# V transposed in bulk beside the last two projection tiles, kept by token in DRAM and loaded per chunk of the scan

## What is computed

```python
z = h @ p['w_in']
...
zc = centred_shift(zc, p['mu'])
r, k, v, lw, la = jnp.split(zc, [W_C, 2 * W_C, 3 * W_C, 3 * W_C + N_DIR * LORA_W], -1)
...
def step(s, inp):
    r_t, w_t, k_t, v_t, kk_t, a_t = inp
    sa = jnp.einsum('bhvk,bhk->bhv', s, kk_t)
    s = (s * w_t[:, :, None, :] - sa[..., None] * (kk_t * a_t)[:, :, None, :]
         + v_t[..., None] * k_t[:, :, None, :])
    return s, jnp.einsum('bhvk,bhk->bhv', s, r_t)
...
out = jnp.concatenate([ya, yb, yc], -1) @ p['w_out']
x = x + gate * rms_norm(out, p['g_post'])
```

## Time and profile before

| | us |
|---|---|
| median of 3 runs | 1105.39 |
| lowest, highest | 1103.64, 1105.43 |
| profiled execution | 1102.38 |
| its span | 1100.7 |
| PE busy | 1007.3 (92%) |
| DVE busy | 644.0 (59%) |
| ACT busy | 427.1 (39%) |
| POOL busy | 406.1 (37%) |

### The profile page before, as it was taken

One profiled execution on the slowest core, in us unless ns is written; L12 is line 12 of the kernel. 1 busy time (PEld: TensorE's weight loads), 2 busy tenths in 40 slices (PEclk: granted clock), 3 DMA queues, 4 the chain that ended last, 5 costly groups with the idle time before them and its releaser, 6 DMA issues. The chain is left out here.

```text
span 1100.7 us, 32049 instructions
## 1 busy us (share of the span) xinstructions
PE 1007.3 (92%) x14407; PEld 907.2 (82%) x14407; DVE 644.0 (59%) x954; ACT 427.1 (39%) x708; POOL 406.1 (37%) x372
## 2 busy tenths in 40 slices
PE   5699999999999999983699989999999997799997
PEld 3299999999989889963699989999899987466685
DVE  5440069585366221343678878888888885356532
ACT  5351201101133343122366655565565652534311
POOL 8111112111206332212556545556666664312200
PEclk9799999999999999995699999999999999989999
DMA  9612422111122110000000000000000000540331
GB/s 355 260 39 82 158 77 78 39 39 39 39 82 82 39 39 1 1 1 10 2 4 4 4 14 4 4 4 4 4 4 4 4 4 4 224 160 26 127 115 58
DMA packets 30036, 61.46 MB, mean 56 GB/s; under 512 B 3352, under 2 KB 21444, under 8 KB 28748
## 3 DMA queue, kind: packets, MB, share of 16 engines
q1 hardware_dynamic: 29900, 59.42, 15.4%
HBM read 49.68 MB, written 9.73 MB: 54 GB/s over the span
## 5 line engine op out<-in xcount | busy, mean ns | idle before, releaser
L681 PE MATMUL ps<-input_rounded,weights_rounded 128*128 128x386 f32 x768 | 263.5, 343 | 4.7 <-DVE input_rest L788 3.3
L683 PE MATMUL ps<-input_rounded,weights_rest 128*128 128x386 f32 x768 | 260.0, 339 | 0.0
L682 PE MATMUL ps<-input_rest,weights_rounded 128*128 128x386 f32 x768 | 259.8, 338 | 0.0
L1412 POOL TENSOR_TENSOR arena<-arena,lvl 128x512 f32<-128x512 f32 x108 | 139.4, 1305 | 76.7 <-ACT arena L1329 46.7
L681 PEld LDWEIGHTS ps<-input_rounded,weights_rounded 128*128 128x128 f32 x768 | 144.7, 188 | 12.1 <-issue 7.5
L470 POOL TENSOR_TENSOR weights_rest<-arena,weights_rounded 128x2048 fp32r<-128x2048 f32 x16 | 75.8, 4740 | 210.7 <-ACT weights_rounded L515 210.7
L682 PEld LDWEIGHTS ps<-input_rest,weights_rounded 128*128 128x128 f32 x768 | 144.8, 189 | 0.5
L683 PEld LDWEIGHTS ps<-input_rounded,weights_rest 128*128 128x128 f32 x768 | 145.0, 189 | 0.0
L1128 PE MATMUL ps<-arena 64*64 64x64 f32 x2880 | 105.4, 223 | 18.0 <-issue 14.7
L1128 PEld LDWEIGHTS ps<-arena 64*64 64x64 f32 x2880 | 93.9, 136 | 23.6 <-issue 17.1
L1138 PE MATMUL ps<-arena 64*64 64x64 f32 x2880 | 105.3, 224 | 5.1 <-DVE arena L1538 4.8
(11 more groups left out here) (247 smaller groups left out, 1705.6 us busy)
## 6 DMA issues: line engine op xcount, KB each, us to landing
arena<-in_w_in SPq DMA_DIRECT2D x16, 1024.0 KB, 5.3
arena<-in_ada_w SPq DMA_DIRECT2D x7, 1024.0 KB, 5.2
mix_scratch<-zc SPq DMA_DIRECT2D x4, 1158.0 KB, 9.6
out<-arena SPq DMA_DIRECT2D x9, 512.0 KB, 3.1
zc<-in_x_sample SPq DMA_DIRECT2D x4, 1024.0 KB, 9.0
hT<-in_ada_w SPq DMA_DIRECT2D x4, 1024.0 KB, 12.0
zc<-in_w_out SPq DMA_DIRECT2D x4, 1024.0 KB, 13.9
arena<-in_x_sample SPq DMA_DIRECT2D x8, 512.0 KB, 3.7
```

Of the source, the lines that this page charges most:

```text
L681: pe.matmul(o, w_hi[:, k, cut], hi_of_h[:, k, cols_b], start=(k == 0), stop=False)
L682: pe.matmul(o, w_hi[:, k, cut], lo_of_h[k][:, cols_b], start=False, stop=False)
L683: last = pe.matmul(o, w_lo[:, k, cut], hi_of_h[:, k, cols_b], start=False, stop=(k == KT - 1))
L1412: pool.tensor_tensor(Um[l % 3], UT, lvl[:, l, :].unsqueeze(1).to_broadcast([P, 2 * PAIRS, C]), ALU.mult).then_inc(q_um[l], 1)
```

## The change

In part 1, PE transposes V in 36 transposes of 128x128, in 12 groups (`V_GROUPS`: channel tile `a`, four, four and one token tiles), two groups behind each of the six column blocks of the last two tiles. The groups go through banks 6 and 7; ACT evicts the even ones and DVE the odd ones, to `v_stage`, which lies on weight slots that are free by then. SP stores each `a` to the DRAM scratch `v_scratch` (token by channel) in two DMAs, and part 1 ends when they have landed. The spread of the key norms waits for all evictions. The reciprocal moves from mix tile 11 to mix tile 9.

In the scan, SP loads `UV[n % 2]` in four DMAs of 64 KB per chunk, once the chunk two before has no more use for it; `transpose_v` and `v_by_token` are gone, `rhs_begin` waits for the load. The lists are put in another order.

```diff
+V_GROUPS = [(a, g) for a in range(4) for g in range(3)]
...
+                for a in range(4):
+                    block = v_stage[a % 2].rearrange("p (i c) -> p i c", i=9)
+                    for by in range(2):
+                        sp.wait_ge(s_vs[by], (3 * a + 4 - by) // 2)
+                    sp.dma_start(v_dram[TP:TP + SEQ, P * a:P * a + P], block[:, 0, :]).then_inc(s_vd[a % 2], 16)
+                    sp.dma_start(v_dram[TS:TS + DEC_SEQ, P * a:P * a + P].rearrange("(i p) c -> p i c", p=P),
+                                 block[:, 1:9, :]).then_inc(s_vd[a % 2], 16)
+                for h in range(2):
+                    sp.wait_ge(s_vd[h], 64)
...
+                def v_by_token(at):
+                    a, g = V_GROUPS[at]
+                    if a >= 2:
+                        act.wait_ge(s_vd[a % 2], 32)
+                    n = min(4, 9 - 4 * g) * P
+                    act.wait_ge(s_vp, at + 1)
+                    act.activation(v_stage[a % 2][:, 512 * g:512 * g + n], ps[:, 6 + at % 2, 0:n], ACT.Copy).then_inc(s_vs[0], 1)
+
                 round_weights(1)
                 for j, kind in enumerate(TILES):
+                    if j >= V_AT:
+                        v_by_token(2 * NB * (j - V_AT))
+                        v_by_token(2 * NB * (j - V_AT) + 2)
...
+                    if j >= V_AT:
+                        v_by_token(2 * NB * (j - V_AT) + 4)
...
+                def transpose_v(at):
+                    a, g = V_GROUPS[at]
+                    pe.wait_ge(s_mix, 9 + a)
+                    if at == 0:
+                        pe.wait_ge(s_kd, NB * PAIRS)
+                    if at >= 2:
+                        pe.wait_ge(s_vs[at % 2], at // 2)
+                    for i in range(4 * g, min(4 * g + 4, 9)):
+                        c = TP if i == 0 else TS + P * (i - 1)
+                        last = pe.transpose(ps[:, 6 + at % 2, P * (i - 4 * g):P * (i - 4 * g) + P], vT[:, a, c:c + P], eye[:, :])
+                    last.then_inc(s_vp, 1)
...
+                    if j >= V_AT:
+                        at = 2 * (NB * (j - V_AT) + b)
+                        transpose_v(at)
+                        transpose_v(at + 1)
...
                 pe.wait_ge(s_kr, 1)
+                for by in range(2):
+                    pe.wait_ge(s_vs[by], len(V_GROUPS) // 2)
...
-                        if i == 11:
+                        if i == 9:
                             dve.wait_ge(s_kd, NB * PAIRS)
                             dve.reciprocal(kn, kn).then_inc(s_kr, 1)
...
+                def load_v(n):
+                    earlier(sp, q_state, n - 1)
+                    earlier(sp, q_yb, n - 1)
+                    for d in DIRS:
+                        rows = v_dram[STARTS[n][d]:STARTS[n][d] + C, :].rearrange("t (a g j) -> t g a j", a=PAIRS, g=2)
+                        for g in range(2):
+                            h = head(d, g, 0)
+                            sp.dma_start(UV[n % 2][OTHER[d], d, h:h + PAIRS, :], rows[:, g]).then_inc(q_vl[n % 2], 16)
...
                     if d == 0:
                         pe.wait_ge(q_x, 4 * (n + 1))
                     else:
-                        pe.wait_ge(q_v, 2 * (n + 1))
+                        earlier(pe, q_m[1], 2 * n)
...
-                    pe.wait_ge(q_v, 2 * (n + 1))
+                    pe.wait_ge(q_vl[n % 2], 64 * (n // 2 + 1))
...
                     if 0 <= n3 < N:
                         copy_u(n3)
+                    if 0 <= n1 < N:
+                        rate(n1)
+                        inverse_decay(n1)
+                        decay(n1)
                     if 0 <= n2 < N:
                         copy_y(n2, 1)
```

More of the change, by code:

```diff
@@ L1088, in lora @@
                     last.then_inc(q_lora, 1)
-                def transpose_v(n):
-                    earlier(pe, q_m[1], 2 * n)
-                    for d in DIRS:
-                        for a, g in HEADS:
-                            last = pe.matmul(ps[OTHER[d], 6 + (g ^ d), C * a:C * a + C], chunk(vT, n, d)[HALVES[g], a, :],
-                                             eyes[HALVES[g], :], start=True, stop=True)
-                    last.then_inc(q_vt, 1)
                 def gram(n, d):
@@ L1226, in _ @@
                 first_state()
-                for step in range(N + 3):
-                    n0, n1, n2, n3 = step, step - 1, step - 2, step - 3
+                for step in range(N + 4):
+                    n1, n2, n3, n4 = step - 1, step - 2, step - 3, step - 4
+                    if 0 <= n3 < N:
+                        product(n3, 2)
+                    if 0 <= n4 < N:
+                        new_state_part(n4)
+                    if 0 <= n3 < N:
+                        update(n3, 2)
+                    if 0 <= n4 < N:
+                        outputs_end(n4)
+                    if 0 <= n3 < N:
+                        product(n3, 3)
@@ L1239, in _ @@
+                    if 0 <= n3 < N:
+                        update(n3, 4)
                     if 0 <= n1 < N:
-                        gram(n1, 0)
+                        lora(n1)
+                    if 0 <= n3 < N:
+                        product(n3, 5)
+                        rhs_begin(n3)
+                        update(n3, 5)
+                        rhs_end(n3)
                     if 0 <= n2 < N:
-                        update(n2, 3)
-                    if 0 <= n1 < N:
-                        gram(n1, 1)
-                        transpose_keys(n1)
+                        product(n2, 1)
@@ L1246, in _ @@
+                    if 0 <= n3 < N:
+                        solve(n3)
                     if 0 <= n2 < N:
[L1247 to L1258 removed]
```

150 lines of the change are left out of this document (68 added, 82 removed).

## The result

| | before | changed |
|---|---|---|
| median of the runs, us | 1104.52 (4 runs) | 1135.45 (4 runs) |
| lowest, highest | 1100.89, 1105.43 | 1134.24, 1136.68 |
| ratio, 95% interval | | 1.029 (1.0267 to 1.0313) |
| span of the profiled execution | 1100.7 | 1133.7 |

A forecast was written before the change was run, and what follows sets the result against it. PE was taken to set the scan's pace, DVE next. Part 1 at +7.2 and the scan at +16.5 (fifteen steps +18, fill -1.5) sum to +23.7: 1126.1 or 1129.1, taken as 1128; range 1099 to 1140.

The forecast's parts named there:

- Part 1: Before the scan: 36 added transposes 4.1 us, spread of key norms 3.1 us later, stores at nothing; +7.2 us.
- The steady step: One step of the scan, summed over four stretches: +1.2 us, 23.4 in place of 22.19, fifteen such steps.
- level 3 to 4: Stretch of PE's step between these products: second gram leaves, transpose_keys waits for the mask; -0.5 us.
- 4 to 5: Stretch of PE's step from level 4 to 5: gram takes the place of transpose_v; +0.15 us.
- 5 to the next level 2: Stretch of PE's step: begin_inverse runs beside POOL's masks, at 1.15 us in place of 0.66; +0.7, bounds +0.1 and +1.2.
- 2 to 3: Stretch of PE's step: all four queries lie beside POOL, 3.35 us in place of 2.43; +0.85, bounds 0 and +0.95.
- The full block: Rival in the scan: begin_inverse waits out a mask, each query one POOL instruction; 22 us more, 1150; chance 0.06.
- The faster rival: Scan: DVE's slowing beside POOL misses the path, PE stays the bound, a step is 21.3 us; 1097 or some 1085; chance 0.17.
- Half of it: Rival in the scan: only the queries or only begin_inverse slowed, +0.35 to +0.5 a step; 1106 to 1115 (chance 0.12 for 1108 to 1115).
- Fill and drain: Scan's start and end: transpose_v leaves the fill's path at half clock, -1.5 us; the drain left as it is.
- What would show it: Signs in the changed profile: step 23.4 us, idle ahead of levels 3 and 1, queries at 0.82 or more, spread 3 us late.

The follow-up runs named there:

- the kernel that fills the gap alone: Lists of before, V loaded, last even group's eviction moved; also transpose_keys behind product of level 4, keys_by_token behind gather_triangle: 1125.19 us, ratio 1.0200 against the kernel before.

## Why the prediction was right, and where it wasn't

**Part 1.** +7.2 predicted, +7.5 measured. The parts are different, and the sum came out by luck. The transposes took 2.94 + 0.71 = 3.65 us to their end in place of 4.1. The wait behind them was 2.33 in place of 3.1: the last five, 0.71 us, run beside ACT's evictions and had been counted in both terms. And 1.4 us, which no term had, is the lower clock of the spread. The cause named, the group's eviction queued behind the last tile's, is shown by the kernel that moves it.

**The steady step.** +1.2 predicted, +1.68 measured, +1.43 in the second half. By stretches: level 3 to 4, -0.45 (-0.5 predicted); 4 to 5, +0.23 (+0.15); 5 to the next level 2, +1.14 (+0.7); 2 to 3, +0.76 (+0.85). The term that was mis-sized is the third. `begin_inverse` was taken at 1.15 us by the ratio that `sum_decays` shows in the earlier trace rows; it took 1.45, and `sum_decays` behind it 1.79 in place of 1.52, which no term had and which held up `factor` and `update` of level 1 (0.17 us). The error is in the model: a ratio was taken for something that is a wait. The fourth stretch came out near for a reason that the model doesn't give: in the changed kernel, as in the earlier trace rows, the queries meet instructions of 256 columns, so that the 0.90 us read there carried over. Where the partner was a mask of 512 columns, it did not. The rule that the runs showed (the rest of POOL's instruction, up to 1.25 us for a mask, plus 0.54) gives 0.66 to 1.79 us by where it falls, with 1.45 well inside.

**The full block.** This rival had the mechanism right. It was given 0.06, against it that "a query beside POOL took 0.90, not 0.41 + 0.75". That was the wrong test. A query waits only for what is left of POOL's instruction. In the earlier trace rows the third query starts at 724.84, POOL's pair ends at 723.94 + 1.51 = 725.45, and the query ends at 725.74: 0.29 later, as in the table. What the Trainium skill says ("SBUF — State Buffer", section "SBUF: two separate sides": whichever starts first holds the pair for the whole instruction, the other fully blocks) is what these runs show, in every case of the table. Only the price put on it, 1150, was too high, since each wait was counted as a whole instruction. That the forecast has the nearer number all the same is in part luck.

**Transpose_v.** The faster rival took its 0.89 us a step as being on the path. It was not: without it, in the old lists, PE waits 0.79 us in the same place. "PE is at 97% today", read in the earlier trace rows, counted a filler as load. The faster rival was dead for that reason, not only for the contention; for the forecast it did no harm, since its stretches were walked one by one.

**Half of it.** Its price, 1106 to 1115, doesn't follow from the prediction's own terms: 15 x 0.35 to 15 x 0.5, with +7.2 and -1.5, is 11 to 13 us, so 1113 to 1119.

**Fill and drain.** -1.5 and 0 predicted. With the old lists the fill did get 2.0 us shorter; with the new ones 0.2. Which waits make up that difference wasn't worked out. The drain is 2.0 longer, all of it in the last two steps, which take 22.38 and 20.05 us where they took 21.48 and 18.90: the prediction had counted the longer steps fifteen times alone. These two terms and the step make up the 9 us between the sum and the two spans.

**What would show it.** The idle time ahead of level 3 (1.31), ahead of level 1 (0.72), `begin_inverse` over 1 us, PE's share (21.27 of 23.87, 89%) and level 4 behind level 3 (4.38) came as said. Three of the four queries are at 0.90, but the first is at 0.72, below the 0.82 said, and the spread starts 2.33 us behind the last transpose, not 3. PE never waits for a load of V; at the scan's start it waits 7.67 us for the loads of the state, before 7.72. The loads of V land in 2.3 us:

```profile
arena<-v_scratch SPq DMA_DIRECT2D x72, 64.0 KB, 2.3
```

## What to carry to other kernels

Before a piece is taken out of a busy engine's list, look at what the instruction behind it waits for: taking out a filler of 0.89 us over a wait of 0.79 is worth nothing until other work is put in its place. Where an instruction of DVE with two inputs in SBUF meets one of POOL, price the meeting as the rest of the other's instruction, not as a slower pace. To tell the two, compare the ends: here one kind of instruction took from 1.51 to 2.23 us and always ended 1.1 us behind its partner. And keep POOL's long instructions away from short ones of DVE that PE waits for. A new list must be followed through every engine, as the chain from POOL's mask over ACT to PE's bank shows, and for the heaviest case of each step.

## What the runs showed of the hardware

A query of 256 columns, 0.41 us alone, took 0.90 beside a pair of POOL's instructions of 256 columns and 1.5 beside one of 512; by its end, it came 0.27 to 0.29 us behind the instruction of POOL that it had met. An instruction of DVE with one input in PSUM, and a transpose with one input in SBUF, took their usual 0.7 us beside the same masks. And the clock fell where PE's waits were short: to 0.57 behind one of 2.33 us in part 1, to 0.62 behind one of 1.40 us in the kernel that fills the gap alone, whereas the changed kernel's step, with waits of 1.31, 0.40, 0.72 and 0.17 us, ran at 1.00 throughout. Why the one and not the other is left open.
